# One two-block transformer kernel on one core: other load order, earlier scores, a split bias table, and a shorter last residual

## The chip, the core and the metric

The kernel runs on one core of a Trainium2 chip. The metric is device time in microseconds (us) of one execution. All data are float32, so every product on TensorE (PE) appears as two instructions in the profile. The other engines are VectorE (DVE), ScalarE (ACT), GpSimd (POOL) and SyncE (SP); SP, ACT and POOL issue DMAs. The memory the engines work in is SBUF; products arrive in PSUM.

## What is computed

256 tokens (2 tiles of 128), width 2048, go through two blocks.

```python
# first block, one layer
h = rms_norm(x, mix_norm_g);  proj = h @ w_in
y_a = causal attention of 16 heads from low-rank latents (rope on 64 of 192 dims)    # "mla"
y_b = causal attention of 16 heads with cumulative log forget gates                  # "fox"
x = x + (concat(y_a, y_b) * sigmoid(gates + b_gate)) @ w_out
h2 = rms_norm(x, ffn_norm_g)
# product keys: per token 8 heads x 16 experts out of 16384, found by two top-16 and a top-16 of sums
x = x + sum_k gate_k * gelu(h2 . peer_u[id_k]) * peer_v[id_k]
# second block, two layers
proj = x @ w_in
ya = difference of two softmaxes (4 heads), yb = dilated windows (8 heads), yc = conv of 31 taps
x = layer_norm(ALPHA * x + concat(ya, yb, yc) @ w_out, ln_g, ln_b)
```

Per tile 128 experts of each token are read twice (`peer_u`, `peer_v`): 256 gathers of 1 MB a tile, 512 in all.

## The kernel before

The order of passes on every engine is: `layer1(0)`, `experts(0)`, `layer1(1)`, `experts(1)`, then `layer2(l, t)` for (0,0), (1,0), (0,1), (1,1); `r = 2t + l + 1` numbers the last four as r = 1, 2, 3, 4. The argument of `layer1` and `experts` is the tile.

**Weights.** SP streams them in order (loop at L904) as units of 1 MB through a ring of four SBUF buffers. A unit is loaded as soon as PE has used the unit four before it. PE multiplies a unit in 4 products of 128x512 (8 instructions, L1242, L1276, L1284).

**Gathers.** POOL issues the 512 gathers in order (L866). Tile 0's need its expert numbers (`ids_ready`, from DVE at L695, in four rounds of 32). A gather goes into one of 6 or 7 row buffers and waits until DVE has used the buffer's last row (`row_used`). DVE uses a row in `slot()` (L356): a dot product with `hrow` (L362) for `peer_u`, a scaled addition to `x_sb` (L370) for `peer_v`. Slots are mixed into the other DVE work of the following passes: `stage(m)` fixes how many slots belong to a stage, `mix(f)` runs them up to the fraction f. DVE works in order, so a wait between two `mix` calls also holds back the slots, the freeing of rows, and POOL.

**experts(t)** (PE L1493, DVE L649, ACT L1100). PE transposes x to `hT`, multiplies it by the query weights in four chunks of four units, transposes each chunk (`keys_T`, L1501) and multiplies it by the sub keys (`scores`, L1510). Within chunk i it does units 0 and 1, `keys_T(i-1)`, units 2 and 3, `scores(i-1)`. DVE writes `hrow`, the normed row that the dot products use, from `x_sb`, the factor `rsh` and the row of gains `grow` (L665), runs the first stage of slots (`mix(1.0)`, none for tile 0, 10 for tile 1), and then takes the scores round by round (L674 to L695). `grow` is loaded once for each tile (`gain_row`, L1098), each time 1 MB, since one row of 8 KB goes to 128 partitions.

**Start.** SP loads tile 0 of x, waits for `k_in` (all constants and columns, L903), and streams the ring. ACT issues `konst`, `cols` and four small inputs (L964). PE's first transposes wait for x and `k_in`. ACT's first activation loads its function table when it comes.

**Second block.** DVE adds the masks `log_count` (`lnc`) to the whole bias table `bias2` at r = 1 (L769, L770). Both were loaded by ACT at the end of `layer1(1)` (L1094). For l = 1 the residual ALPHA * x enters the accumulation in PSUM by 16 products of `hT` with ALPHA times the identity (`residual()`, L1542). At a layer's end `add_out` (L519) takes each bank of 512 columns from PSUM, reduces it (L535) and sums the first three; ACT squares x minus a shift in two pieces (L1192, L1194); `layer_stats` (L541) makes mean and variance in five small operations, ACT takes the root (L1198), DVE the reciprocal (L554). At r = 3, ACT also loads the two rows of gains of the last norm (L1138, L1139, 1 MB each).

## Time and profile before

| | |
|---|---|
| median of 3 runs | 3245.87 us (3245.82 to 3246.41) |
| the profiled execution | 3247.37 us, its span 3245.6 us |
| PE busy | 2493.9 us (77%), 6764 instructions |
| DVE busy | 1670.2 us (51%) |
| ACT busy | 480.4 us (15%) |
| POOL busy | 938.7 us (29%) |
| bytes moved | 1192.41 MB, mean 367 GB/s |

The span begins with the first instruction and ends with the last; 1.77 us of the execution lie outside of it. A busy share is a mean over stages with different limits, so a change is weighed in the stage in which it lies: until about 580 us PE streams weights alone, to about 2642 us the gathers run beside it, and after that PE streams alone again. An instruction row of the trace gives start, duration, engine, line, what it writes and reads, and in brackets the idle time before it with what ended it.

### The profile page before, as it was taken

What the parts mean: (1) busy time and instruction counts of PE and PEld (TensorE: products, weight loads), DVE (VectorE), ACT (ScalarE), POOL (GpSimd) and SP (SyncE); (2) the same over time, 40 slices, a digit from 0 to 9 for tenths busy, and PEclk for the clock granted to TensorE, in tenths of its full rate; (3) what the DMA queues carried; (4) which work ended last, traced back from release to release, by engine and by line L of the source; (5) the groups of instructions that cost most, each with busy time, mean ns of one, the idle gap of its engine ahead of it and who ended that gap; (6) DMA issues with size and microseconds to landing.
All of it is one profiled execution on the core that took longest, in us unless ns stands there. A gap on an engine that the chain in (4) does not pass through costs nothing.

```text
span 3245.6 us, 19086 instructions
## 1 busy us (share of the span) xinstructions
PE 2493.9 (77%) x6764; PEld 1190.4 (37%) x6764; DVE 1670.2 (51%) x2188; ACT 480.4 (15%) x1159; POOL 938.7 (29%) x643
## 2 busy tenths in 40 slices
PE   8999999946847867576888267555745689999998
PEld 4444444413323333233433123222322234444553
DVE  1101112977576676676798956675985641011211
ACT  3222222111101111111101001010100011111211
POOL 0000000254354353343323334442342315300800
PEclk9999999977968878787999698778978899999999
DMA  8788787999999999999999999999999998887776
GB/s 319 268 294 279 271 285 273 394 421 421 421 416 420 422 419 422 422 417 422 410 421 421 405 422 422 421 415 422 421 402 422 421 392 284 280 287 268 269 265 220
DMA packets 166174, 1192.41 MB, mean 367 GB/s; under 512 B 18488, under 2 KB 18744, under 8 KB 21952
## 3 DMA queue, kind: packets, MB, share of 16 engines
q1 hardware_dynamic: 90320, 644.13, 52.6%
q0 software_dynamic: 73872, 537.95, 40.0%
q10 hardware_dynamic: 1888, 9.11, 0.7%
q8 instruction: 54, 0.88, 0.1%
q14 instruction: 40, 0.33, 0.0%
HBM read 1189.02 MB, written 2.10 MB: 367 GB/s over the span
## 4 chain that ended last, share of the span: by engine, by line
PE 40%; DMA 37%; DVE 14%; POOL 5%; issue 4%; ACT 1%; DVEq 0%; ACTq 0%
PE psP L1242 27%; DMA rows<-in_peer_v,tk 19%; DMA rows<-in_peer_u,tk 15%; PE psO L1276 6%; POOL rows L866 4%; DVE x_sb L370 4%; DVE rows L362 3%; DMA ring<-in_w 2%; PE psO L1284 2%; DVE work L386 1%; PE psX L1335 1%; PE psX L1332 1%; PE psX L1331 1%; POOL hrow L866 1%; DMA hrow<-in_peer_u,tk 1%
## 5 line engine op out<-in xcount | busy, mean ns | idle before, releaser
L1242 PE MATMUL psP<-ring,hT 128*128 128x512 f32 x3584 | 1633.0, 609 | 113.2 <-DMA ring<-in_w 106.1
L1242 PEld LDWEIGHTS psP<-ring,hT 128*128 128x128 f32 x3584 | 682.3, 195 | 978.8 <-issue 799.5
L866 POOL DMA_INDIRECT rows<-in_peer_u,tk x222 | 351.8, 1585 | 1091.8 <-DVEq L695 580.2
L370 DVE SCALAR_TENSOR_TENSOR x_sb<-rows,tk,x_sb 128x2048 f32<-128x2048 f32 x223 | 524.3, 2351 | 240.5 <-DMA rows<-in_peer_v,tk 220.4
L362 DVE CUSTOM_DVE_ANT_0 rows<-rows,hrow 128x2048 f32<-128x2048 f32 x222 | 503.9, 2290 | 193.7 <-DMA rows<-in_peer_u,tk 189.1
L866 POOL DMA_INDIRECT rows<-in_peer_v,tk x223 | 337.6, 1514 | 554.6 <-DVE x_sb L370 496.6
L1276 PE MATMUL psO<-ring,work 128*128 128x512 f32 x832 | 388.2, 620 | 0.5 <-DMA ring<-in_w 0.5
L1276 PEld LDWEIGHTS psO<-ring,work 128*128 128x128 f32 x832 | 162.3, 201 | 186.8 <-issue 186.0
L1368 PE MATMUL psX<-kst,work 128*128 128x128 f32 x128 | 26.9, 348 | 251.7 <-DVEq L517 194.9
L981 ACT ACTIVATE work<-work,small 128x256 f32<-128x256 f32 (+1 forms) x128 | 56.6, 443 | 482.9 <-DVEq L496 482.9
L514 DVE SCALAR_TENSOR_TENSOR work<-psX,small,work 128x128 f32<-128x128 f32 x96 | 27.0, 344 | 191.7 <-PE psX L1358 191.3
L1242 PE MATMUL psP<-ring,work 128*128 128x512 f32 (+1 forms) x288 | 114.8, 547 | 7.3 <-DMA ring<-in_w 7.3
L1368 PEld LDWEIGHTS psX<-kst,work 128*128 128x128 f32 x128 | 19.2, 176 | 273.1 <-DVEq L517 204.0
L370 DVE SCALAR_TENSOR_TENSOR x_sb<-hrow,tk,x_sb 128x2048 f32<-128x2048 f32 x33 | 77.6, 2351 | 36.5 <-DMA hrow<-in_peer_v,tk 33.1
L362 DVE CUSTOM_DVE_ANT_0 hrow<-hrow 128x2048 f32<-128x2048 f32 x34 | 77.8, 2290 | 28.1 <-DMA hrow<-in_peer_u,tk 27.4
L1335 PE MATMUL psX<-kv,work 128*128 128x128 f32 x128 | 28.0, 341 | 81.2 <-DVE kv L503 81.2
L1284 PE MATMUL psO<-ring,work 128*128 128x512 f32 x192 | 87.1, 611 | 1.7 <-ACT work L994 1.4
L866 POOL DMA_INDIRECT hrow<-in_peer_u,tk x34 | 54.5, 1604 | 89.1 <-DVE tk L362 67.9
L885 POOL TENSOR_TENSOR work<-work 128x512 f32<-128x512 f32 x60 | 76.2, 1271 | 4.7
L1242 PEld LDWEIGHTS psP<-ring,work 128*128 128x128 f32 x288 | 53.5, 190 | 64.7 <-issue 61.3
L866 POOL DMA_INDIRECT hrow<-in_peer_v,tk x33 | 50.0, 1517 | 85.6 <-DVE x_sb L370 73.4
L386 DVE SCALAR_TENSOR_TENSOR work<-work,cols 128x128 f32<-128x128 f32 x240 | 68.0, 346 | 0.0
(334 smaller groups left out, 1606.6 us busy)
## 6 DMA issues: line engine op xcount, KB each, us to landing
ring<-in_w SPq DMA_DIRECT2D x572, 1024.0 KB
ring<-in_wq SPq DMA_DIRECT2D x32, 1024.0 KB
ring<-in_w SPq DMA_DIRECT2D x8, 512.0 KB
rows<-in_peer_v,tk POOLq DMA_INDIRECT x223
rows<-in_peer_u,tk POOLq DMA_INDIRECT x222
x_sb<-in_x SPq DMA_DIRECT2D x2, 1024.0 KB, 6.4
rows<-in_gate_bias SPq DMA_DIRECT2D x1, 2048.0 KB, 12.7
work<-in_sub_keys ACTq DMA_DIRECT2D x2, 1024.0 KB, 9.2
```

The costliest lines, as they stand in the source:

```text
L362: V.tensor_tensor_reduce(out=row_buf(n), in0=row_buf(n), in1=hrow[:, t, :], scale=1.0, scalar=0.0, op0=ALU.mult, op1=ALU.add, accum_out=do ...
L370: V.scalar_tensor_tensor(out=x_sb[:, t, :], in0=row_buf(n), scalar=dots[t][:, k:k + 1], in1=x_sb[:, t, :], op0=ALU.mult, op1=ALU.add).then ...
L386: own.add(V.scalar_tensor_tensor(out=cacc[:, c, :], in0=convh[:, c, k:k + P], scalar=w, in1=cacc[:, c, :], op0=ALU.mult, op1=ALU.add))
L866: pool.indirect_dma_start(out=row_buf(n), out_offset=None, in_=a["peer_u" if s < SLOTS else "peer_v"], in_offset=bass.IndirectOffsetOnAxis ...
L885: own.link(T(cacc, cacc, csq, ALU.add))
L981: ins = A(W4[:, j, :], W4[:, j, :], ACT.Exp, bias=negm[:, 4 * u + j:4 * u + j + 1], accum_out=lsum[:, 4 * u + j:4 * u + j + 1])
L1242: last = MM(psP[:, c % 2, 0:wide], src[:, kk, :], w[:, k, :], start=(kk == 0 and not begun), stop=(kk == 4 * nu - 1))
L1276: last = MM(psO[:, d, :], src[:, k, :], w[:, d, :], start=(bool(first) and k == 0), stop=False)
L1284: last = MM(psO[:, d, :], src[:, k, :], w[:, k, :], start=False, stop=(k == 3))
L1331: MM(o, qT[:, j, :], kT[:, j, :], start=True, stop=False)
L1335: last = MM(o, qT[:, j, :], kT[:, j, :], start=(kind != "fox"), stop=(kind != "fox" or bank_ends))
L1368: last = TR(psX[:, 0, P * j:P * (j + 1)], mN[:, P * j:P * (j + 1)], ident)
```

## The change

1. Start: ACT loads only the identity and 16 columns first (`first_in`) and makes one activation of a constant that DVE has set (`booted`). The rest of `konst` and `cols` and the four small inputs are issued by POOL after x is there. SP no longer waits before the ring.
2. `experts`: `keys_T(i-1)` comes after one unit of chunk i and `scores(i-1)` after two. For tile 1, PE transposes `hT` back to rows in chunk 1 (`rows_back`), and DVE writes `hrow` from PSUM, before the first `mix`; the second load of `grow` is gone.
3. Bias table: columns 128 to 255 are loaded and masked where all were; columns 0 to 127 are loaded by ACT at r = 3 and masked by DVE there. ACT loads two more rows (gain and offset of layer 0's norm) behind them.
4. Tile 1's residual: at r = 3 DVE multiplies x by ALPHA, at r = 4 by ALPHA and the gains, and adds the offset; `residual()` is for tile 0 alone.
5. Statistics: for tile 1 addition and sum are one instruction; the second piece of the squares enters in ACT's root.

```diff
@@ vector
+                    sum_ = msum[:, d:d + 1]
+                    if t == 1:
+                        link(V.tensor_tensor_reduce(out=xv, in0=xv, in1=psO[:, d, :], scale=1.0, scalar=0.0, op0=ALU.add, op1=ALU.add,
+                                                    accum_out=sum_))
+                        dve.sem_inc(x_added, 1)
                     else:
...
-                link(V.tensor_scalar(vart[:, 1:2], nm, sh, None, ALU.subtract))
...
-                link(V.tensor_scalar(var, ssl[:, 0:1], ssl[:, 1:2], 1.0 / D, ALU.add, ALU.mult))
-                link(V.tensor_scalar(var, var, vart[:, 1:2], 1e-5, ALU.add, ALU.add))
+                link(V.scalar_tensor_tensor(out=bias, in0=ssl[:, 0:1], scalar=1.0 / D, in1=dev, op0=ALU.mult, op1=ALU.add))
...
                 take_xT(split, "ffn_g", (2, 3))
-                dve.wait_ge(grow_in, 16 * (t + 1))
                 dve.wait_ge(rsx_ready, t + 1)
+                if t == 0:
+                    dve.wait_ge(grow_in, 16)
                 for d in range(4):
                     w = slice(512 * d, 512 * (d + 1))
+                    if t == 1:
+                        dve.wait_ge(h2T_done, d + 1)
+                        V.tensor_scalar(hrow[:, 1, w], psX[:, d % 2, :], rsh[:, 1:2], None, ALU.mult).then_inc(h2T_taken, 1)
+                        continue
...
                 own.own()
+                if t == 1:
+                    dve.wait_ge(h2T_taken, 4)
                 mix(1.0)
...
                     layer_end(1, 0, 2)
+                    link(V.tensor_scalar(x_sb[:, 1, :], x_sb[:, 1, :], ALPHA, None, ALU.mult))
+                    dve.wait_ge(bias_in, 64)
+                    add_mask(slice(0, P), lnc_far)
+                if r == 4:
+                    link(V.scalar_tensor_tensor(out=x_sb[:, 1, :], in0=x_sb[:, 1, :], scalar=ALPHA, in1=ln_g0, op0=ALU.mult, op1=ALU.mult))
+                    link(V.scalar_tensor_tensor(out=x_sb[:, 1, :], in0=ln_b0, scalar=ALPHA, in1=x_sb[:, 1, :], op0=ALU.mult, op1=ALU.add))
@@ gpsimd
+            pool.wait_ge(x_in, 16)
+            pool.dma_start(kst[:, P:NKONST], a["konst"][:, P:NKONST]).then_inc(k_in, 16)
+            pool.dma_start(cols[:, DC:NCOLS], a["cols"][:, DC:NCOLS]).then_inc(k_in, 16)
+            for dst, name in ((rowc[:, :], "rowc"), (posi, "positions"), (dlam, "diff_lambda"), (work[32:40, 8448:9984], "gate_bias")):
+                pool.dma_start(dst, a[name]).then_inc(in_in, 16)
@@ sync
             sp.dma_start(x_sb[:, 0, :], a["x"][:, 0, :]).then_inc(x_in, 16)
-            sp.wait_ge(k_in, 32)
@@ scalar
+                act.dma_start(kst[:, 0:P], a["konst"][:, 0:P]).then_inc(first_in, 16)
+                act.dma_start(cols[:, 0:DC], a["cols"][:, 0:DC]).then_inc(first_in, 16)
+                act.wait_ge(booted, 1)
+                own.link(A(vart[:, 5:6], vart[:, 4:5], ACT.Copy))
...
-                    gain_row(1)
-                    act.dma_start(bias2, a["bias_t"]).then_inc(bias_in, 16)
-                    act.dma_start(lnc, a["log_count"]).then_inc(bias_in, 16)
+                    act.dma_start(bias2[:, :, P:S], a["bias_t"][:, :, P:S]).then_inc(bias_in, 16)
+                    act.dma_start(lnc, a["log_count"][:, :, P:S]).then_inc(bias_in, 16)
...
+                    act.dma_start(bias2[:, :, 0:P], a["bias_t"][:, :, 0:P]).then_inc(bias_in, 16)
+                    act.dma_start(lnc_far, a["log_count"][:, :, 0:P]).then_inc(bias_in, 16)
+                    for dst, name, at_ in ((ln_g, "ln_g", D), (ln_b, "ln_b", D), (ln_g0, "ln_g", 0), (ln_b0, "ln_b", 0)):
+                        act.dma_start(dst, bass.AP(tensor=a[name].tensor, offset=at_, ap=[[0, P], [1, D]])).then_inc(lnrow_in, 16)
...
-                A(vart[:, 2:3], vart[:, 0:1], ACT.Sqrt).then_inc(sd_ready, 1)
+                A(vart[:, 2:3], ssl[:, 1:2], ACT.Sqrt, scale=1.0 / D, bias=vart[:, 0:1]).then_inc(sd_ready, 1)
@@ tensor
-                    units(c, 0, 2, 4, hT)
-                    keys_T(i - 1)
-                    units(c, 2, 4, 4, hT)
-                    scores(i - 1)
+                    units(c, 0, 1, 4, hT)
+                    if t == 1 and i == 1:
+                        rows_back(0, 2)
+                        units(c, 1, 2, 4, hT)
+                        rows_back(2, 4)
+                        pe.wait_ge(h2T_taken, 4)
+                        keys_T(0)
+                        units(c, 2, 3, 4, hT)
+                        scores(0)
+                        units(c, 3, 4, 4, hT)
+                    else:
+                        keys_T(i - 1)
+                        units(c, 1, 2, 4, hT)
+                        scores(i - 1)
+                        units(c, 2, 4, 4, hT)
...
+                    for j in range(4):
+                        last = TR(psX[:, r % 2, P * j:P * (j + 1)], hT[:, 4 * r + j, :], ident)
+                    last.then_inc(h2T_done, 1)
...
-                        if l and g == 1:
+                        if l and t == 0 and g == 1:
                             residual()
```

## Rows read from the trace of the kernel before

**Rows 1.** The page's second part: GB/s moved in 40 equal slices.

```profile
GB/s 319 268 294 279 271 285 273 394 421 421 421 416 420 422 419 422 422 417 422 410 421 421 405 422 422 421 415 422 421 402 422 421 392 284 280 287 268 269 265 220
```

**Rows 2.** Stretches: us, busy of PE, PEld, DVE, ACT, POOL; clock, DMA share, GB/s.

```profile
560.00:580.00 20.00, 20.00 (x63) 10.13 (x62) 15.84 (x62) 1.97 (x3) 0.00 (x0) 1.00 0.82 280
1600.00:1700.00 100.00, 79.03 (x197) 34.95 (x196) 94.63 (x233) 9.53 (x14) 37.38 (x19) 0.95 1.01 422
580.00:2640.00 2060.00, 1338.59 (x3468) 629.51 (x3466) 1477.92 (x1748) 233.82 (x581) 793.95 (x512) 0.84 1.01 418
```

**Rows 3.** Waits over the span: who waited for what, us in total, times, longest.

```profile
DVE x_sb L370 <- DMA rows<-in_peer_v,tk: 220.4, 101, 2.7
```

**Rows 4.** Timeline of the start: start us, us, engine, line, operation, count, idle before.

```profile
7.42 25.29 SPq L909 DMA_DIRECT2D ring<-in_w  x9
7.51 1.57 PEld L1254 LDWEIGHTS psX<-kst,x_sb 128*128 128x128 f32 x8 [7.51 <-DMA x_sb<-in_x]
8.72 1.28 ACT L959 ACT_TABLE_LOAD   x1 [8.72 <-PE psX L1254]
12.31 0.50 PEld L1242 LDWEIGHTS psP<-ring,hT 128*128 128x128 f32 x2 [0.39 <-DMA ring<-in_w]
28.96 0.69 ACT L1013 ACTIVATE work<-psP,small 128x512 f32<-128x512 f32 x1 [4.76 <-PE psP L1242]
```

**Rows 5.** Timeline of `experts(0)`: first scores, DVE's copy of them, first gather.

```profile
562.12 1.05 PE L1510 MATMUL psO<-work 128*128 128x128 f32 x8
563.29 0.69 DVE L674 COPY rows<-psO 128x512 f32<-128x512 f32 x1 [21.67 <-PE psO L1510]
580.61 1.16 POOL L866 DMA_INDIRECT rows<-in_peer_u,tk  x1 [580.16 <-DVEq L695]
```

**Rows 6.** Timeline of `experts(1)`: PE, DVE and POOL up to the first scores.

```profile
1549.51 17.43 PE L1242 MATMUL psP<-ring,hT 128*128 128x512 f32 x40
1553.82 2.74 DVE L665 SCALAR_TENSOR_TENSOR hrow<-x_sb,small,kv 128x512 f32<-128x512 f32 x4 [8.21 <-ACTq L1117]
1556.59 17.09 DVE L370 SCALAR_TENSOR_TENSOR x_sb<-rows,tk,x_sb 128x2048 f32<-128x2048 f32 x7
1559.21 3.00 POOL L866 DMA_INDIRECT rows<-in_peer_v,tk  x1 [34.19 <-DVE x_sb L370]
```

**Rows 7.** Stretches around POOL's stop in `experts(1)`, columns as in rows 2.

```profile
1550.00:1555.00 5.00, 5.00 (x13) 2.28 (x12) 1.19 (x2) 3.60 (x7) 0.00 (x0) 1.00 1.01 422
1560.00:1565.00 5.00, 5.00 (x13) 2.19 (x12) 4.79 (x3) 0.69 (x1) 4.39 (x3) 1.00 1.01 324
```

**Rows 8.** DVE's waits from 1756 to 1800 us: us in total, times, longest.

```profile
DVE rows L362 <- DMA rows<-in_peer_u,tk: 10.5, 7, 1.6
DVE hrow L362 <- DMA hrow<-in_peer_u,tk: 2.3, 2, 1.5
```

**Rows 9.** Timeline: starved ring, then r = 3; last a load's KB and us to landing.

```profile
1583.58 3.70 PE L1242 MATMUL psP<-ring,hT 128*128 128x512 f32 x8 [0.84 <-DMA ring<-in_wq]
1588.57 3.70 PE L1242 MATMUL psP<-ring,hT 128*128 128x512 f32 x8 [1.29 <-DMA ring<-in_wq]
...
2650.09 58.76 PE L1242 MATMUL psP<-ring,hT 128*128 128x512 f32 x136
2675.61 0.69 DVE L741 TENSOR_TENSOR work<-work 128x512 f32<-128x512 f32 x1 [16.06 <-ACT work L1141]
...
rows<-in_ln_b ACTq DMA_DIRECT2D x1, 1024.0 KB, 11.1
```

**Rows 10.** Timeline of the boundary from r = 3 to r = 4, and `residual()`.

```profile
2934.81 0.69 DVE L535 TENSOR_REDUCE small<-x_sb 128x1 f32<-128x512 f32 x1
2937.81 1.38 PE L1254 MATMUL psX<-kst,x_sb 128*128 128x128 f32 x8 [3.87 <-DVE x_sb L819]
2940.99 5.76 PE L1242 MATMUL psP<-ring,hT 128*128 128x512 f32 x8
3082.06 3.74 PE L1545 MATMUL psO<-kst,hT 128*128 128x128 f32 x32
```

More of the change, by code:

```diff
@@ L264, in build @@
         bias2 = v3(kv[:, 6144:9216], S)
-        lnc = v3(kv[:, 2048:2560], S)
+        lnc = v3(kv[:, 2048:2304], P)
+        lnc_far = v3(rows[:, 4, 0:256], P)
         eid = [tk[:, 384 * t:384 * t + P].bitcast(U32) for t in range(TT)]
@@ L272, in build @@
         topk_home = [rows[:, NB - 1, :], kv[:, 0:2048]]
-        grow = [rows[:, NB - 1, :], kv[:, 4096:6144]]
+        grow = rows[:, NB - 1, :]
         skT = v3(wk(3840, 5888), NK)
-        ln_g, ln_b = rows[:, 0, :], rows[:, 1, :]
+        ln_g, ln_b, ln_g0, ln_b0 = (rows[:, m, :] for m in range(4))
         def row_buf(n):
@@ L544, in layer_stats @@
-                link(V.tensor_scalar(nm, msum[:, 3:4], part3[:, t:t + 1], 1.0 / D, ALU.add, ALU.mult))
-                link(V.tensor_scalar(vart[:, 1:2], nm, sh, None, ALU.subtract))
-                link(V.scalar_tensor_tensor(out=vart[:, 1:2], in0=vart[:, 1:2], scalar=-1.0, in1=vart[:, 1:2], op0=ALU.mult, op1=ALU.mult))
+                nm, sh, dev, bias = nmean[:, t:t + 1], shift[:, t:t + 1], vart[:, 1:2], vart[:, 0:1]
+                link(V.tensor_scalar(nm, msum[:, 3:4], part3[:, t:t + 1], -1.0 / D, ALU.add, ALU.mult))
@@ L557, in layer1 @@
                 stage(MIX1[0] if t else 0)
+                if t == 0:
+                    V.memset(vart[:, 4:5], 1.0).then_inc(booted, 1)
+                    dve.wait_ge(first_in, 32)
                 take_xT(split, "mix_g")
@@ L712, in finish_rows, with add_mask @@
                 dve.sem_inc(x_final, 1)
+            def add_mask(w, count):
+                own.add(V.tensor_tensor(bias2[:, 0:4, w], bias2[:, 0:4, w], over(count[:, 0, :], 4), ALU.add))
+                link(V.tensor_tensor(bias2[:, 4:12, w], bias2[:, 4:12, w], over(count[:, 1, :], 8), ALU.add))
             def apply_ln(t):
                 if t == 0:
-                    dve.wait_ge(lnrow_in, 32)
+                    dve.wait_ge(lnrow_in, 64)
                 for d in range(4):
@@ L768, in layer2 @@
                         dve.wait_ge(bias_in, 32)
-                        own.add(V.tensor_tensor(bias2[:, 0:4, :], bias2[:, 0:4, :], over(lnc[:, 0, :], 4), ALU.add))
-                        link(V.tensor_tensor(bias2[:, 4:12, :], bias2[:, 4:12, :], over(lnc[:, 1, :], 8), ALU.add))
+                        add_mask(slice(P, S), lnc)
                     mix(at_kT)
@@ L1192, in layer_squares @@
                 own.add(A(junk[:, 0:1536], x_sb[:, t, 0:1536], ACT.Square, bias=shift[:, t:t + 1], accum_out=ssl[:, 0:1]))
-                act.wait_ge(x_added, 8 + 4 * r)
-                own.add(A(junk[:, 1536:2048], x_sb[:, t, 1536:2048], ACT.Square, bias=shift[:, t:t + 1], accum_out=ssl[:, 1:2]))
                 own.own()
                 act.sem_inc(sq_done, 1)
+                act.wait_ge(x_added, 8 + 4 * r)
+                own.link(A(junk[:, 1536:2048], x_sb[:, t, 1536:2048], ACT.Square, bias=shift[:, t:t + 1], accum_out=ssl[:, 1:2]))
                 act.wait_ge(var_ready, r)
-                A(vart[:, 2:3], vart[:, 0:1], ACT.Sqrt).then_inc(sd_ready, 1)
+                A(vart[:, 2:3], ssl[:, 1:2], ACT.Sqrt, scale=1.0 / D, bias=vart[:, 0:1]).then_inc(sd_ready, 1)
             def y_count(l, t):
```

48 lines of the change are left out of this document (27 added, 21 removed).

## The prediction

> **What bounds the kernel now.** I read the page's slices first, then the stretches, then the waits, then the timeline at each place that the change touches. The slices show three stages [rows 1]. Up to slice 7 the DMAs move 268 to 319 GB/s and in the last seven slices 220 to 287; there PE streams weights and the transfers keep up. Between them, from 580 to 2640 us, they move 418 GB/s on average, in the busy stretches 421 to 422 [rows 2]; 422 is the most this kernel gets. DVE waits 220 us for rows of peer_v alone, 101 times [rows 3]. So the middle is a matter of bytes: 512 gathers and the ring share one pipe, and the stage ends when all of it is moved. There time is lost only where the pipe isn't full, and gained only where bytes go or where the pipe had room. DVE is a close second in places, 94.6% busy from 1600 to 1700 us [rows 2]. In the first and third stage a microsecond on PE's path is a microsecond of the total; a shift at the start moves everything behind it.
>
> **1, the start.** Now SP's ring, PE and DVE begin at 7.4 to 7.5 us, when x and all constants are there: 2.0 MB have come together [rows 4]. PE's first product of weights starts at 12.31, 4.8 us later; 1.28 us of that is ACT's table load, which sits between PE's first transposes and the first copy of them. After the change x is first in SP's queue with the ring behind it, and only 72 KB come beside it on ACT's. The nearest row for "first of several 1 MB loads on an idle queue" is the ring's first unit: issued at 7.42, landed by 12.31, 4.89 us [rows 4]. x, issued at 0.75, is then there at 5.6. Add 4.8 - 1.28 = 3.5 us: first product at 9.2, with unit 0 landed about 2.5 us behind x (1.05 MB at 422 GB/s), at 8.2. Gain 3.1 us. Bounds: 1.3 us if x lands no earlier than now and only the table load goes; 3.6 as the best. The Trainium skill, page "DMA: Bandwidth & Descriptors", section "Anatomy of one DMA", gives a fixed 2.0 us plus bytes over 436 GB/s for a load issued by GpSimd; as an estimate that is 4.4 us for x and would make the gain 3.6, while the row has 4.9, which I take. POOL's six loads (0.9 MB) start behind x. Who waits for them: DVE's rope work and ACT's Ln, behind which ACT's copies of PE's chunks are queued. The loads should land by 13 to 14 us (0.9 MB at half the pipe behind x), and ACT has 4.76 us of idle time before the first copy, at 28.96 [rows 4]; beyond that each microsecond is one of PE's. POOL has nothing else to do until 580. SP's later loads (x of tile 1, gate bias) keep their place.
>
> **2a, scores earlier in experts(0).** The first scores start at 562.12 [rows 5] and move two units up. A unit is 8 of the 136 instructions that take 58.76 us [rows 9], 3.46 us, so they move by 6.9, less the small waits of the transposes: 6.7. DVE idles 21.67 us for them and POOL waits for DVE's first round, so the first gather goes from 580.6 to 573.9. But from 560 to 580 us the pipe carries 280 GB/s [rows 2], so starting early uses (422 - 280) x 6.7 = 0.95 MB of room, 2.2 us. The other 4.5 us of lead only let the gathers take from the ring what they give back later. Bounds 0 and 6.7; I take 2.2. In experts(1) the earlier scores bring nothing: DVE takes them behind its ten slots.
>
> **2b, hrow of tile 1 from PSUM.** This is the part that costs. Now DVE waits for the factor until 1553.8, writes hrow in 2.74 us, and starts the slots at 1556.6; POOL, stopped for 34.2 us, resumes at 1559.2 [rows 6]. After the change the last two pieces come from rows_back(2, 4), behind two units of chunk 1. PE's 40 instructions from 1549.5 are the last three units of chunk 0 and two of chunk 1 [rows 6]; the first of chunk 1 ends at 1563.4. Add eight transposes (1.1 us, as the eight instructions of the scores in rows 5), a unit (3.4), four transposes (0.5), two copies from PSUM (1.4, as DVE's in rows 5): the slots begin at 1570. All behind it on DVE, and POOL behind DVE, is 13.4 us late. With gathers stopped the pipe falls from 422 to 324 GB/s [rows 7], or 280 with the ring alone [rows 2]; 13.4 us at 98 to 142 GB/s less is 1.3 to 1.9 MB, 3.1 to 4.5 us; I take 4.0. DVE's own lag of 13.4 us is not the price as long as DVE gets it back: from 1600 to 1700 it has little room, but from 1756 to 1800 it waits 12.8 us for rows [rows 8]. Bounds: 0, if later stretches with room in the pipe take it up (418 against 422 over 2060 us is 20 us of room [rows 2]), and 13.4. PE's 16 added transposes (2 us) lie where PE is starved.
>
> **3, bytes moved out.** grow's 1 MB and half of bias and mask (0.9 MB), together 2.0 MB or 4.7 us of pipe, leave the middle stage. They were moved while the gathers stood: the pipe is full to 1555 with them [rows 7], and PE ran without waiting for the ring. Take them away and it runs dry sooner; nothing else is ready to be moved. I count 0; bounds 0 and -4.7. DVE's two mask operations halve (1.8 us less at 1708), within a stretch whose time goes to row waits later: 0.
> At r = 3 ACT now issues 5.1 MB at once instead of 2.1. Two queues share evenly: with gathers beside it PE gets a unit every 5.0 us (3.70 busy, 1.29 waiting), against 3.4 used, and this starvation first shows about 23 us after the gathers resume [rows 6, 9]. The 2.1 MB of before landed within 11.1 us and PE's 136 instructions ran through [rows 9]. 5.1 MB at 210 GB/s take 24 us, 1.5 more than the ring holds out, at (5 - 3.4)/5 lost: 0.5 us. The half tables come in pieces of 512 bytes, which no row shows. If they cost double it is 28.5 us and 1.8 us lost. I take 0.9, bounds 0 and 4. The Trainium skill, "DMA: Bandwidth & Descriptors", section "Specifications", has 512 B as the least size at line rate; by it the term would be 0.5. DVE's new wait for the table has the gate of the convolution behind it, which now comes at 2675.61 after 16 us of idle time; PE asks for it behind the 136 instructions, at 2708.8: 33 us of cover [rows 9].
>
> **4, the residual.** 32 instructions, 3.74 us [rows 10], a little overlapped with their neighbours, on PE's path with nothing beside it: -3.6. DVE's added multiplications (2.4 us each, as one of the seven in rows 6) lie ahead of the same gate as above, under the same cover.
>
> **5, statistics.** At the end of r = 3 and r = 4 the reduction (0.69 us and its gap, L535) leaves the chain from the last bank to PE's restart at 2937.81 [rows 10]; five small operations stay five. 0.7 us each, -1.4. PE then idles 3.2 instead of 3.87 us; its clock fell to 1.2 GHz behind that gap and the first unit took 5.76 instead of 3.43 [rows 10]. If the shorter gap spares that, 2.3 more; I don't count it.
>
> **Sum.** -3.1 - 2.2 + 4.0 + 0 + 0.9 - 3.6 - 1.4 = -5.4 us. The terms are from the profiled execution of 3247.37 us, 1.5 above the median; from the median, 3245.87 - 5.4 = **3240.5 us**.
>
> **Rivals.** (a) DVE, not the pipe, carries the middle: the 13.4 us of 2b arrive whole. It decides if DVE isn't rid of its lag by 1800, when its row waits end. For it: DVE busy 94.6% in the stretch behind [rows 2]. Against: the 12.8 us [rows 8]. 3240.5 + 9.4 = 3249.9, slower than before; with the long burst of part 3, 3253. (b) The same for 2a: the 6.7 us arrive whole, 3236.0. Against: the row waits [rows 3], which a full pipe makes. (c) The 2.0 MB do count, since the rows that are under way at the stop land sooner and later dips take the rest: 3235.8. (d) x lands no earlier because the ring behind it crowds it, so the start does not do what it says: only the table load is gained, 3242.3.
>
> **Chances.** Forecast 0.45, (a) 0.20, (b) 0.12, (c) 0.13, (d) 0.10. 0.2% (6.5 us) is about what a measurement of this kernel tells from no change. Faster than 3239.4: (b), (c) and two fifths of the forecast's case, 0.42; slower than 3252.4: half of (a) and a little for what I don't see, 0.13; between them 0.45. Range 3232 (b or c together with a little more) to 3251 (a).
>
> **What the profile after would show.** PE's first L1242 at about 9.2 us. POOL's first gather some 10 us earlier than 580.6. In experts(1) POOL idle some 13 us longer than 34, and a stretch near 280 to 320 GB/s for 25 us around it; then DVE without row waits until it has caught up, or, by (a), x_final and everything behind it 13 us late relative to the start of the pass. No wait for the ring around 2680, or a few of 1.3 us. L1545 only for tile 0. The gap of PE between r = 3 and r = 4 down to 3.2 us. I am wrong if the whole stretch of the gathers, now some 2060 us [rows 2], differs by more than 5 us from the +8.5 that the terms give (first gather earlier by 6.7, less 2.2, plus 4.0).

## The result, and the profile after

The changed kernel takes 3252.06 us (median of 22 runs, 3246.89 to 3259.22) where the kernel before takes 3246.28 us in the same session (22 runs, 3243.59 to 3251.68). The ratio is 1.0018, with a 95 % interval of 1.0011 to 1.0024: 5.8 us slower. I had said 3240.5, range 3232 to 3251. The profiled execution took 3250.77 us, its span 3248.9 us, against 3247.37 and 3245.6 us for before. These two lie 3.4 us apart and the medians 5.8 (after's execution is 1.3 us below its median, before's 1.1 above), so the rows below account for 3.4 us; the other 2.4 us have no rows.

| Where | before, us | after, us | loss (+) or gain (-) of the stage |
|---|---|---|---|
| first transposes of experts(0) | 531.4 | 528.4 | -3.0 |
| first gather | 580.6 | 570.7 | (9.9 earlier) |
| first transposes of experts(1) | 1543.0 | 1537.2 | -2.8 |
| x of tile 0 final, layer2(0,0) begins | 1620.1 | 1627.7 | +13.3 |
| r = 3 begins | 2644.4 | 2646.8 | -5.1 |
| r = 4 begins | 2937.8 | 2946.5 | +6.3 |
| end of the span | 3245.6 | 3248.9 | -5.4 |

Two places lose: experts(1), and r = 3. Each has its rows.

The start. Timeline after (start us, us, engine, line, operation, count, idle before), which answers to [rows 4]:

```profile
1.19 0.45 ACTq L1000 DMA_DIRECT2D cols<-in_cols  x1
1.67 1.28 ACT L1002 ACT_TABLE_LOAD   x1 [1.67 <-PEq L1812]
8.81 1.94 PE L1289 MATMUL psX<-kst,x_sb 128*128 128x128 f32 x8 [8.81 <-DMA cols<-in_cols]
12.12 4.18 PE L1277 MATMUL psP<-ring,hT 128*128 128x512 f32 x8
```

The loads of the first 30 us after (KB, us from issue to landing):

```profile
x_sb<-in_x SPq DMA_DIRECT2D x1, 1024.0 KB, 5.2
kst<-in_konst ACTq DMA_DIRECT2D x1, 64.0 KB, 5.4
cols<-in_cols ACTq DMA_DIRECT2D x1, 8.0 KB, 7.5
```

x, issued at 0.75, is there at 5.95, 0.35 us behind the forecast. But PE waits until 8.8 for 8 KB of `cols`. The first product starts at 12.12, not at 9.2; what is gained is that ACT's table load is out of the way and that the first unit takes 4.18 us instead of the 5.87 in the same view of before. That this is TensorE's clock is a guess from the durations: the profile's rows grant 1.00 in both kernels from 12 to 18 us, and over the kernels below the first unit took 3.9 to 5.6 us with part 1 and 4.7 to 6.3 without, so single values say little.

The middle. Timeline after, first gather and experts(1), which answers to [rows 5, 6]:

```profile
1521.73 16.12 ACTq L1128 DMA_DIRECT2D kv<-in_log_count  x1
1537.89 0.63 ACT L1138 ACTIVATE hrow<-x_sb 128x512 f32<-128x512 f32 x1 [16.61 <-issue]
1540.96 0.63 PE L1289 MATMUL psX<-kst,x_sb 128*128 128x128 f32 x4 [2.75 <-issue]
1559.03 1.04 PE L1576 MATMUL psX<-kst,hT 128*128 128x128 f32 x8
1563.98 1.41 DVE L679 TENSOR_SCALAR hrow<-psX,small 128x512 f32<-128x512 f32 x2 [2.82 <-PE psX L1576]
1568.10 3.00 POOL L894 DMA_INDIRECT rows<-in_peer_v,tk  x1 [47.87 <-DVE x_sb L371]
```

POOL stands for 47.9 us, 13.7 more than in [rows 6], about as forecast, though by luck in part, since it has a second cause. The first line was not forecast: ACT's instruction that issues the load of the counts takes 16.12 us. The same load took ACT 0.45 us in before. (16.61 us is ACT's idle time before its first square; `issue` means that the profile shows nothing it waited for.) All ACT work of experts(1) is behind it, and PE waits 2.75 us for ACT's copies between its x transposes (0.84 in before).

What that does to the pipe, in stretches of after (us, busy of the engines, clock, DMA share, GB/s):

```profile
1540.00:1590.00 50.00, 47.97 (x147) 23.86 (x148) 23.31 (x14) 11.11 (x27) 17.68 (x8) 1.00 0.85 313
1590.00:1700.00 110.00, 80.70 (x207) 36.39 (x206) 102.55 (x272) 9.23 (x13) 39.26 (x21) 0.92 1.01 414
1540.00:1700.00 160.00, 128.68 (x353) 60.26 (x354) 125.87 (x285) 20.34 (x40) 56.95 (x29) 0.95 0.96 382
```

and the same 160 us of before:

```profile
1540.00:1700.00 160.00, 134.22 (x351) 60.78 (x350) 133.30 (x303) 21.64 (x43) 54.86 (x29) 0.97 1.01 416
```

(416 - 382) GB/s x 160 us = 5.4 MB were not moved. 1.97 MB of them (gain row, half table, half counts) no longer had to be, so 3.5 MB are owed to the rest of the middle stage: at 422 GB/s 8.2 us. Measured from the first transposes of experts(1) to the start of r = 3, after takes 1109.6 us and before 1101.4: 8.2 us. From x_final (x of tile 0 complete) to r = 3 after is the quicker by 5.1 us; both kernels move 418 GB/s there, so after simply has fewer bytes left, having moved more of them in its longer experts(1).

Then r = 3. Timeline of PE after, which answers to the third line of [rows 9] (there 136 instructions without a wait):

```profile
2677.74 3.67 PE L1277 MATMUL psP<-ring,hT 128*128 128x512 f32 x8 [1.07 <-DMA ring<-in_w]
2682.63 3.70 PE L1277 MATMUL psP<-ring,hT 128*128 128x512 f32 x8 [1.22 <-DMA ring<-in_w]
2688.85 29.43 PE L1277 MATMUL psP<-ring,hT 128*128 128x512 f32 x64 [2.52 <-DMA ring<-in_w]
```

4.8 us in three waits; behind the last the granted clock, 1.00 from 2660 to 2685, is 0.86 over ten microseconds (2690 to 2700), and the 64 instructions take 29.43 us where 64 of the 136 in [rows 9] take 27.65: 1.8 us. The sum, 6.6 us, less the 0.7 of the shorter statistics, is the stage's loss but for 0.4 us. The loads that shared the pipe with the ring (r = 3 of after; KB, median us from issue to landing):

```profile
rows<-in_ln_g ACTq DMA_DIRECT2D x2, 1024.0 KB, 18.1
rows<-in_ln_b ACTq DMA_DIRECT2D x2, 1024.0 KB, 22.5
kv<-in_bias_t ACTq DMA_DIRECT2D x1, 768.0 KB, 5.7
```

The last boundary, which answers to [rows 10]:

```profile
2946.51 1.11 PE L1289 MATMUL psX<-kst,x_sb 128*128 128x128 f32 x8 [3.14 <-DVE x_sb L847]
2949.69 4.84 PE L1277 MATMUL psP<-ring,hT 128*128 128x512 f32 x8
```

The gap is 3.14 us instead of the 3.87 of before, as forecast. The unit behind it takes 4.84 us instead of 5.76: the 0.9 us of clock that the forecast named and didn't count. The granted clock in before is 0.50, the level of 1.2 GHz, from 2940 to 2944 us. Over the ten microseconds behind the gap (the third number from the end) it is, before and then after:

```profile
2938.00:2948.00 10.00, 9.09 (x27) 4.85 (x27) 3.26 (x10) 3.01 (x8) 0.00 (x0) 0.66 0.09 16
2947.00:2957.00 10.00, 8.81 (x28) 4.64 (x27) 4.10 (x11) 3.01 (x8) 0.00 (x0) 0.83 0.19 52
```

### The profile page after: what moved, and what is told of

Read it like the earlier page. It is cut to its first block, busy times and chain, and to the rows that moved or that the text cites. A ratio compares the mean times of both kernels' runs of the same rounds, so it can differ in the third digit from the quotient of the medians.

```text
span 3248.9 us, 19075 instructions
## 1 busy us (share of the span) xinstructions
PE 2484.9 (76%) x6748; PEld 1186.3 (37%) x6748; DVE 1668.8 (51%) x2194; ACT 481.0 (15%) x1160; POOL 933.4 (29%) x649
## 4 chain that ended last, share of the span: by engine, by line
DMA 18%; PE 18%; DVE 11%; issue 3%; POOL 2%; ACT 0%; DVEq 0%; ACTq 0%
PE psP L1277 13%; DMA rows<-in_peer_v,tk 10%; DMA rows<-in_peer_u,tk 7%; DVE x_sb L371 3%; PE psO L1311 3%; DVE rows L363 2%; POOL rows L894 2%; DVE work L387 1%; PE psO L1319 1%; DMA ring<-in_w 1%; DMA hrow<-in_peer_u,tk 1%; DVE hrow L363 1%; PE psX L1393 0%; POOL hrow L894 0%; DVE kv L651 0%
## 5 line engine op out<-in xcount | busy, mean ns | idle before, releaser
L894 POOL DMA_INDIRECT rows<-in_peer_u,tk x222 | 344.0, 1549 | 1085.6 <-DVEq L713 561.0
L1289 PE MATMUL psX<-kst,x_sb 128*128 128x128 f32 x112 | 20.4, 329 | 65.8 <-DVE x_sb L847 33.6
```

The source lines that it names most:

```text
L894: pool.indirect_dma_start(out=row_buf(n), out_offset=None, in_=a["peer_u" if s < SLOTS else "peer_v"], in_offset=bass.IndirectOffsetOnAxis ...
```

## The experiments

Each was timed in 11 runs (two of them in 8 and 10) against runs of the kernel before on the same chip; times are medians, ratios come with their 95 % intervals. An interval reaches about 3 us to either side, so a difference of medians under 3 us can't be told from nothing by the times alone. The last three columns are from one profiled execution of each kernel. A kernel named "only" is the kernel before with one part of the change; one named "no" is the changed kernel without that part. Two columns of the table that follows carry the argument: "slots", from experts(1)'s first transposes to DVE's first slot behind the stop, and "middle", from the same point to the start of r = 3. The two profiled kernels have 13.6 and 1101.4 (before), 28.3 and 1109.6 (after).

| Kernel | Parts | us (before beside it) | ratio | slots | middle | r = 3 |
|---|---|---|---|---|---|---|
| only_1 | 1 | 3246.1 (3247.4) | 0.9996 [0.9987, 1.0005] | 13.6 | 1103.2 | 293.4 |
| only_2a | 2a | 3245.3 (3247.1) | 0.9991 [0.9982, 1.0000] | 13.6 | 1102.8 | 293.2 |
| only_2b | 2b | 3253.2 (3247.0) | 1.0020 [1.0010, 1.0029] | 26.8 | 1107.7 | 293.7 |
| only_3 | 3 | 3255.6 (3247.4) | 1.0027 [1.0018, 1.0036] | 22.4 | 1110.7 | 294.3 |
| counts_first | 3, other order | 3247.3 (3246.7) | 0.9998 [0.9989, 1.0007] | 13.6 | 1102.5 | 294.3 |
| only_45_late | 4, 5 | 3240.5 (3247.1) | 0.9983 [0.9974, 0.9992] | 13.6 | 1100.6 | 292.4 |
| no_2b | 1, 2a, 3, 4, 5 | 3250.2 (3247.0) | 1.0008 [0.9999, 1.0017] | 24.0 | 1111.7 | 297.2 |
| no_3 | 1, 2, 4, 5 | 3247.9 (3247.0) | 1.0004 [0.9995, 1.0013] | 26.4 | 1109.7 | 295.8 |
| rows_late | all, loads spread | 3247.2 (3247.0) | 0.9996 [0.9987, 1.0005] | 30.9 | 1113.6 | 292.4 |
| early_whole | 1, 2, 4, 5, 2b earlier | 3240.5 (3247.1) | 0.9976 [0.9967, 0.9985] | 19.8 | 1107.2 | 293.7 |
| sum_1_2a_45 | 1, 2a, 4, 5 | 3238.2 (3247.1) | 0.9975 [0.9966, 0.9984] | 13.6 | 1102.1 | 292.5 |
| sum_swap | the same, start swapped | 3238.1 (3247.4) | 0.9971 [0.9962, 0.9980] | 13.6 | 1103.0 | 292.5 |
| sum_hold | the same, ring held | 3237.5 (3247.4) | 0.9971 [0.9962, 0.9981] | 13.6 | 1102.2 | 292.4 |
| all_mended | all, four mendings | 3238.8 (3246.7) | 0.9974 [0.9964, 0.9985] | 19.5 | 1103.1 | 292.4 |

The "middle" of one execution isn't sharp: the eight kernels with slots at 13.6, before among them, spread from 1100.6 to 1103.2, and a single number of that column means no more than that.

**Undoing 2b or 3.** no_2b loads the gain row again and writes hrow of tile 1 the old way; no_3 loads table and counts whole in layer1(1):

```
-                    if t == 1:
-                        dve.wait_ge(h2T_done, d + 1)
-                        V.tensor_scalar(hrow[:, 1, w], psX[:, d % 2, :], rsh[:, 1:2], None, ALU.mult).then_inc(h2T_taken, 1)
-                        continue
+                    gain_row(1)
```

> The changed kernel with 2b undone: hrow of tile 1 again from x, gain row and factor, the gain row loaded again (1 MB). Theory H (the longer stop of POOL empties the pipe): POOL's stop goes from 47.9 back to about 34 us, x_final comes 6 to 8 us earlier, of which some 2 are given back by 2640 us; the total falls by 5 us, to 3247. Rival P (the loads in pieces of 512 bytes hold ACT and the pipe, so the stop matters little): x_final moves by 2 us at most and the 1 MB costs 2.4 us, total 3251 to 3253.

```
-                    act.dma_start(bias2[:, :, P:S], a["bias_t"][:, :, P:S]).then_inc(bias_in, 16)
+                    act.dma_start(bias2, a["bias_t"]).then_inc(bias_in, 16)
```

> The changed kernel with part 3 undone: the whole bias table and counts are loaded in layer1(1) in rows of 1 KB and up, 4.2 MB in whole rows are left at the start of r = 3. Theory P (pieces of 512 bytes cost more than their bytes): ACT is no longer held for 16 us behind its issue at 1521, PE's x transposes in experts(1) wait 2 us less, and r = 3 loses nothing to the ring (4.2 MB at 210 GB/s take 20 us, less than the ring's 23 us of reserve): total down by 8, 3244. Rival B (the bytes of the burst count, not their pieces): r = 3 still waits for the ring about 3 us instead of 4.8 and the total falls by 2 to 3, to 3249.5; the 0.9 MB more in the middle could take 2 of that back.

Taken away singly, neither brings what theory H or P wanted. Against before they are 3.2 and 0.9 us slower where the changed kernel is 5.8, so 2.6 and 4.9 us are gained, each give or take 3 us. no_2b shows why. Its slots still come 10.4 us late, although rows_back is gone: with the gain row queued too, ACT is held for 20.95 us and PE waits 8.58 us between its x transposes. Theory H expected x_final 6 to 8 us earlier and POOL's stop at 34; they were 4.4 and 43.1. no_3 frees ACT (its three issues take 0.33 to 0.45 us again) and halves r = 3's waits, but 2b's own lag stays, slots at 26.4. Its ring waits, 2.6 us, are about what rival B said (3). The two faults delay the same slots, so taking one away leaves most of the lag that the other makes. The middle of no_3 is as long as after's (1109.7 and 1109.6 us): in the changed kernel, what the hold of ACT costs the middle is about what the 0.9 MB spared by part 3 give it. The waits of PE over r = 3 of no_3, with 4.2 MB of whole rows at its start:

```profile
PE psP L1272 <- DMA ring<-in_w: 2.6, 2, 1.4
```

**The burst of r = 3.** rows_late issues the four rows behind the gates of groups 0 and 1, so that only the half table and counts stand at the start:

```
+                    if r == 3 and g < 2:
+                        for dst, name, at_ in (((ln_g, "ln_g", D), (ln_b, "ln_b", D)), ((ln_g0, "ln_g", 0), (ln_b0, "ln_b", 0)))[g]:
+                            act.dma_start(dst, bass.AP(tensor=a[name].tensor, offset=at_, ap=[[0, P], [1, D]])).then_inc(lnrow_in, 16)
```

> The changed kernel with the four rows of gain and bias (4.2 MB) issued one and two groups later in r = 3, so that only the half table and counts (0.9 MB in pieces of 512 bytes) come at its start. Theory B (bytes): no wait for the ring and no fall of the clock at r = 3, 6.3 us less, 3246. Theory P (pieces): the half table alone still starves the ring, PE waits 1 to 3 us and the gain is about 3 to 4 us, 3248.5. In either case the time up to 2646 us is that of the changed kernel within 1 us.

Theory B: r = 3 takes 292.4 us instead of 299.7, without a wait for the ring. PE's 136 instructions run through, with 0.9 MB in pieces of 512 bytes in front of them:

```profile
2656.50 58.53 PE L1278 MATMUL psP<-ring,hT 128*128 128x512 f32 x136
```

So it is mostly the bytes, one kernel for each amount: 2.1 MB (before) no wait, 3.0 MB (only_3) 0.8 us, 4.2 MB (no_3) 2.6 us, 5.1 MB (after) 4.8 us. The total fell by 5.6 us against before's. The middle of the profiled execution was 4 us longer than after's, where I had expected 1 us: ACT was held for 16.93 us and the slots came at 30.9.

**Each part alone.**

> The kernel before with 2b alone: hrow of tile 1 from PSUM behind two units of chunk 1, the gain row of tile 1 not loaded. Theory H: POOL's stop grows by 9 to 14 us, x_final comes 7 us later and the total rises by 4 to 6 us, to 3251. By my blind sum (the pipe's loss alone) it rises by 4.0, to 3250. Rival P: the stop is harmless without the loads in pieces, total within 1.5 us of before.

2b alone costs 6.2 us, where theory H had 4 to 6. Its stretch and its restart:

```profile
1540.00:1700.00 160.00, 130.79 (x364) 61.59 (x362) 125.63 (x282) 20.60 (x40) 56.08 (x29) 0.95 0.97 394
1570.00:1575.00 5.00, 5.00 (x19) 2.79 (x18) 4.79 (x3) 0.00 (x0) 3.91 (x2) 1.00 0.45 133
```

22 GB/s less over 160 us is 3.5 MB, less 1.05 MB that needn't be moved: 2.5 MB or 5.9 us; the middle is 6.3 us longer. The slots come 13.1 us late, by the prediction 13.4. What I had wrong is the rate while the gathers stand: not 280 to 324 GB/s throughout, but, in steps of 5 us from 1550, 318, 282, 323 and then 267 and 133. The low steps are those in which PE does transposes and waits (3.94 us busy of 5 from 1565) and in which the first gather behind the stop has only just been issued (1570.8); that these are the reasons is argued, not tested.

> Part 3 alone on the kernel before: half of the bias table and counts at the start of r = 3, both halves in pieces of 512 bytes. Theory P: ACT is held 15 to 21 us by the issue of the counts at 1527 (0.45 in before), PE's second x transposes in experts(1) wait 3 to 9 us instead of 0.8, DVE's slots begin 4 to 8 us later than 1556.6 and x_final as much; at r = 3 3.0 MB (0.9 in pieces) cost nothing or one wait of 1.3 us; total 3249 to 3252. Rival: the 0.9 MB less in the middle pay for the hold (-2.2 us), total within 1.5 us of before.

Part 3 alone costs 8.2 us, the most of all. The prediction had 0.9, and the total is beyond the text above too (3249 to 3252; 3255.6). Timeline of ACT in only_3:

```profile
1525.27 0.63 ACTq L1101 DMA_DIRECT2D kv<-in_bias_t  x1
1525.93 21.05 ACTq L1102 DMA_DIRECT2D kv<-in_log_count  x1
1547.03 0.63 ACT L1112 ACTIVATE hrow<-x_sb 128x512 f32<-128x512 f32 x1 [22.02 <-issue]
```

> Part 1 alone on the kernel before. Blind sum: first product at 9.2 us and 3.1 us less, 3243.5. By the changed kernel's trace: first transposes at 8.8 to 9.2 us (the 8 KB of cols land 7.5 us after their issue), first product at 12.1 to 12.5 as before, but at a faster clock, experts(0) begins some 2 us earlier, and the total falls by 1 to 2 us, to 3245.5; rival: the pipe in the middle swallows this too, 0.

1.3 us, which can't be told from nothing. The eight kernels with part 1 and the ring not held begin experts(0) at 528.0 to 529.0 us, the six without it, before among them, at 529.1 to 532.6: 2.2 us between the means. The 3.1 of the prediction was too much.

> Part 2a alone on the kernel before: scores one unit behind the queries in both experts passes. The first gather comes 6.5 to 7 us earlier, at 574. Blind sum: only the pipe's room counts, -2.2, 3244. Rival: the 6.7 us arrive whole, 3239.5. Second rival: the ring waits it causes and the dips later take all of it, 0, 3246.5.

The first gather is at 574.89, 5.7 us ahead of [rows 5] although this execution began experts(0) 1.2 us later, so 6.9 earlier by itself. The median gains 1.8 us (forecast: 2.2); the interval reaches from 0 to 5.8 us, so it rules out the rival of 6.7 but not the one of 0. The rows do: from the first transposes of experts(0) to those of experts(1) the ten kernels with 2a take 1008.5 to 1010.7 us, the six without it 1011.1 to 1012.2, 2.7 us between the means.

> Parts 4 and 5 alone on the kernel before, the rows of gain and bias issued one and two groups later in r = 3 (the changed kernel needs two more of them). By the blind sum -3.6 for the residual and 0.7 for each of two boundaries, -5.0: 3241.5. With what the changed kernel's trace shows at the clock (first product behind the gap 4.8 us instead of 5.8) -6: 3240.5. Rival: the added multiplications on DVE or the rows' loads delay the gate of the convolution or take the pipe, and no more than 3 us are left: 3243.5.

6.6 us by the medians, 5.5 by the ratio, against 5.0 in the prediction. The r = 3 to r = 4 boundary of this kernel:

```profile
2934.21 1.11 PE L1269 MATMUL psX<-kst,x_sb 128*128 128x128 f32 x8 [3.14 <-DVE x_sb L833]
2937.39 4.85 PE L1257 MATMUL psP<-ring,hT 128*128 128x512 f32 x8
```

It is 3.14 and 4.85 us here too, where before has 3.87 and 5.76: the shorter gap is followed by a shorter stretch at 1.2 GHz, 0.9 us that I had left out of the sum.

**What holds ACT.** By then the open point was whether the pieces hold ACT or the order. counts_first is only_3 with the counts issued ahead of the other loads and the half table behind them all:

```
+                if t:
+                    act.dma_start(lnc, a["log_count"][:, :, P:S]).then_inc(bias_in, 16)
                 act.dma_start(skT, a["sub_keys"]).then_inc(sk_in, 16)
...
                     act.dma_start(bias2[:, :, P:S], a["bias_t"][:, :, P:S]).then_inc(bias_in, 16)
-                    act.dma_start(lnc, a["log_count"][:, :, P:S]).then_inc(bias_in, 16)
```

> Part 3 alone on the kernel before, as in only_3, but the 128 KB of counts are issued first of ACT's four loads at the end of layer1(1) and the half table in pieces of 512 bytes last, so that no load is issued behind it. Theory Q (an issue behind a load in many pieces holds ACT until that load is under way): no issue longer than 1 us, ACT's first square of experts(1) at the time of before, PE's second transposes wait 0.8 us again, slots by 1555, total 5 to 7 us below only_3, 3249.5 (0.8 and its clock left at r = 3). Rival R (the pieces themselves hold ACT, wherever they stand): the hold of 16 to 21 us moves to the issue of the table or of the gain row, total 3255 again.

```profile
1526.57 0.63 ACTq L1099 DMA_DIRECT2D kv<-in_log_count  x1
1527.24 0.61 ACTq L1100 DMA_DIRECT2D work<-in_sub_keys  x1
1527.88 0.45 ACTq L1106 DMA_DIRECT2D kv<-in_ffn_row  x1
1528.37 0.55 ACTq L1103 DMA_DIRECT2D kv<-in_bias_t  x1
```

Theory Q, and 2 us better than it had. The same four loads, the same pieces, and no issue over 0.63 us; the slots are back at 13.6, and 8.2 us have become 0.6. So one load issued behind the half table costs 8 us here, and the half table itself nothing that these runs can tell. The table lands 28.8 us after its issue, twice the bytes in whole rows took 22.3 in before; nobody waits for it.

The order alone isn't the condition, though. At r = 3 the other half of the table, again 768 KB in pieces of 512 bytes, has loads issued behind it in six kernels, and ACT is not held there. From after:

```profile
2661.42 0.56 ACTq L1171 DMA_DIRECT2D kv<-in_bias_t  x1
2662.00 0.73 ACTq L1172 DMA_DIRECT2D rows<-in_log_count  x1
2663.41 1.51 ACTq L1174 DMA_DIRECT2D rows<-in_ln_b  x1
```

1.51 us is the longest issue at r = 3 in any kernel. The table lands 5.7 to 5.9 us after its issue at r = 3, and 23.0 to 25.6 in the four kernels that hold ACT: there the sub keys, and in two of them the gain row, are ahead of it on ACT's queue and the pipe is full (422 GB/s from 1550 to 1555 in before [rows 7]), while at r = 3 nothing of ACT's is ahead of it and the pipe has room (294 GB/s from 2660 to 2665 in after). The hold is also longer where the gain row (1 MB) goes ahead of the table (20.95 and 21.05 us) than where it doesn't (16.12 and 16.93). So what the runs show is that the issue behind a load in many pieces waits where that load itself is slow to get moving. Which limit it waits at they don't show.

**Moving rows_back forward.** early_whole has part 3 undone, the rows spread, and the two halves of rows_back behind the third and the fourth unit of chunk 0:

```
                     units(c, q, q + 1, 4, hT)
+                    if back_to and q == 2:
+                        pe.wait_ge(*back[3])
+                        back_to(0, 2)
+                    if back_to and q == 3:
+                        back_to(2, 4)
```

> The changed kernel with the bias table loaded whole in layer1(1) (3 undone), the rows of gain and bias later in r = 3, and rows_back(0, 2) and rows_back(2, 4) put behind the third and the fourth unit of chunk 0, so that DVE's slots in experts(1) start about 7 us earlier (1556.5 instead of 1563.3 with 3 undone). Theory H: x_final 5 to 7 us earlier than 1627.3, r = 3 begins 2 to 4 us earlier than 2646.6, no ring wait: total 3239 to 3241. Rival: the stop of POOL is not what 2b costs (the 1 MB that is not moved and the dips behind it level it), r = 3 begins at 2646 again and only the ring wait is gained: 3244.

The slots came at 19.8 instead of no_3's 26.4, x_final 8.2 us sooner, the total at 3240.5. The profiled execution began r = 3 only 1.8 us sooner than no_3's, less than theory H asked; its stretch 1540 to 1700 moved 408 GB/s, by which the middle should be under 1 us longer than before's and not 5.8. Where those 5 us went I don't know.

**The start.** sum_1_2a_45 leaves out 2b and 3 and spreads the rows; the two others change its start alone.

> Parts 1, 2a, 4 and 5 alone on the kernel before: 2b and 3 undone, and the four rows of gain and bias issued one and two groups later in r = 3. If the loss of the changed kernel sits in 2b, in the pieces of 512 bytes and in the burst, and the rest adds up (start -3.0, tail -5.4 as read from the traces, 2a between 0 and -2.2), x_final comes by 1618 us, no ring wait at r = 3, and the median falls 8 to 10 us below before, to 3237.5. Rival: the middle gives back what the start and 2a bring, since its end is a matter of bytes that are moved at 418 GB/s in any case and the earlier gathers only take from the ring; then r = 3 starts at 2642 to 2644 and the total is 5 us below before, 3241.5.

9.0 us below before: the parts alone give 1.3 + 1.8 + 6.6 = 9.7. The rival, that the middle swallows the gains (5 us), lies just outside the interval of 5.2 to 11 us.

```
-                act.dma_start(kst[:, 0:P], a["konst"][:, 0:P]).then_inc(first_in, 16)
                 act.dma_start(cols[:, 0:DC], a["cols"][:, 0:DC]).then_inc(first_in, 16)
+                act.dma_start(kst[:, 0:P], a["konst"][:, 0:P]).then_inc(first_in, 16)
```

> Parts 1, 2a, 4 and 5 as in the sum kernel, with ACT's first two loads in the other order: the 8 KB of cols (pieces of 64 bytes) issued at 0.75, the 64 KB of konst at 1.2. Theory C (what is issued at 1.2 us lands behind the ring's first unit, whatever its size): konst lands at 8.7 and nothing is gained, first transposes at 8.8 to 9.1, total 3238. Theory D (the pieces of 64 bytes are slow by themselves, 7.5 us from issue): cols lands at 8.3, konst at 6.6, first transposes at 8.3 to 8.6, total 3237.5. If neither, both land with x at 6 to 6.5, first product at 9.7 and the total is 2 us lower, 3236.

```profile
kst<-in_konst ACTq DMA_DIRECT2D x1, 64.0 KB, 7.7
cols<-in_cols ACTq DMA_DIRECT2D x1, 8.0 KB, 5.5
```

```
             sp.dma_start(x_sb[:, 0, :], a["x"][:, 0, :]).then_inc(x_in, 16)
+            sp.wait_ge(first_in, 32)
```

> Parts 1, 2a, 4 and 5 as in the sum kernel, with SP's ring held until the two first loads have landed, so that only x is beside them. Theory C (crowded by the ring's first unit): cols lands at about 6.3 instead of 8.7, first transposes at 6.3, the ring's first unit is issued then and is there 4.9 us later, at 11.2, which is when the first product starts (12.4 in the sum kernel); total 1 us lower, 3237. Theory D (slow pieces): cols lands at 8.5 again, the ring's first unit at 13.5, and the total is 1 us higher, 3239.5.

```profile
6.89 1.94 PE L1280 MATMUL psX<-kst,x_sb 128*128 128x128 f32 x8 [6.89 <-DMA cols<-in_cols]
11.77 5.37 PE L1268 MATMUL psP<-ring,hT 128*128 128x512 f32 x8 [1.36 <-DMA ring<-in_w]
```

Theory C twice over. Swapped, the two loads swap their times: whatever is issued at 1.2 us, 8 KB or 64, lands 7.5 to 7.9 us later, behind the ring's first unit, which was issued at 1.19 too. With the ring held both need 5.6 us and the transposes start at 6.9. Then the ring's unit is the late one, and the first product comes 0.6 us sooner than in sum_1_2a_45. The median is 0.5 us below that of sum_swap on the same chip, which these runs can't tell from nothing. sum_hold is the fastest kernel of the study, 3237.5 us, 0.9971 of before.

**All parts, mended.** Ring held, counts first, rows_back forward, rows spread:

> All parts of the changed kernel with four things mended: SP's ring held until the two first loads are there, the counts issued ahead of the half table, rows_back behind the third and fourth unit of chunk 0, the four rows of gain and bias one and two groups later in r = 3. Theory Q: slots begin at about 1556, no ring wait at r = 3, total as that of early_whole with the start of sum_hold, 3239.5. If the 1 MB and 0.9 MB that it doesn't move in the middle count after all (4.7 us), 3236. Theory R: ACT is held again, slots at 1562 or later, total 3243.

3238.8 us, between the 3239.5 and the 3236 of theory Q; the four mendings were not tried one by one. Slots 5.9 us late, and yet the middle is only 1.7 us longer than before's: 12 GB/s less over 1540 to 1700 is 1.92 MB, and 1.97 MB needn't be moved. sum_hold, without 2b and 3, is at 3237.5 with an interval that overlaps: even mended, 2b and 3 bring nothing that can be told from nothing.

## Why the prediction was wrong

The steps that failed are the landing of `cols` at the start, the rate at which 2b loses bytes, the issue on ACT that part 3 makes slow, and the length and price of the burst at r = 3. In the order of the terms:

- **1, the start** (-3.1; measured -1.3 alone). x and the ring's first unit landed when they should (5.95 and 8.5 us for 5.6 and 8.2). The step that failed is "only 72 KB come beside it": I took them as there with x because they are small. They landed last, at 8.7 us, and the first product stayed at 12.1 instead of 9.2. (The prediction also has DVE begin at 7.4 to 7.5 us; in before it begins at 9.5, which no term uses.) Rival (d) had the ring crowd x; it crowded `cols`.
- **2a** (-2.2; measured -1.8 by the median, -2.7 by the rows). Right: most of the 6.7 us of lead doesn't arrive. That it is the pipe's room between 560 and 580 us that counts fits, and was not tested by itself.
- **2b** (+4.0; measured +6.2 alone). The delay was right (13.1 for 13.4 us), and so was pricing it by missing bytes; the rate at which bytes go missing was mis-sized. In the terms of the sum: 3.5 MB missing less 1.05 saved, where I had 1.3 to 1.9 MB.
- **3, bytes** (0, bounds 0 and -4.7). Where both parts are in and 1.97 MB are spared, the stretch gives the middle only if they are taken off: 8.2, 12.8 and -0.1 us for after, rows_late and all_mended, measured 8.2, 12.2 and 1.7; without taking them off it would be 4.7 us more each. For 0.9 or 1.05 MB alone it stays open: only_2b (5.9 with them taken off, 8.3 without, measured 6.3) and no_3 (7.7, 10.2 and 8.3) speak for it, only_3 (7.7, 9.9 and 9.3), no_2b (7.7, 9.9 and 10.3), counts_first (-1.0, 1.1 and 1.1) and early_whole (0.5, 3.0 and 5.8) against. And nothing was left of the saving, since the stops that came with it cost more. I had written that the ring "runs dry sooner; nothing else is ready to be moved", and that is the other side of the same account.
- **3, the issue on ACT** (not in the sum; alone worth the 8.2 us of only_3 less the 0.6 of counts_first). This wait the prediction had at nothing without a reason. It asked what a moved DMA does to the ring and never what its issue does to ACT's own queue. Each issue of before takes 0.33 to 0.45 us there, and the prediction gave the issue no price at all. In the changed kernel it overlaps with 2b: without it (no_3) the slots come 26.4 instead of 28.3 us behind the first transposes.
- **3, the burst at r = 3** (+0.9, bounds 0 and 4; measured about 6.6 with the clock). Three sizes failed. I let the ring hold out 23 us, as it did behind POOL's restart; it held out 15, from the issue at 2661.4 to the first wait at 2676.7. The 23 us were a poor measure: in the first 15 us behind POOL's restart the ring of before was given 3.40 MB, at r = 3 of after 3.03 MB, and until its first wait before's PE did 2.2 us of transposes and scores, which use no unit. (Nothing shows that after's ring was behind when the burst came: its units issued at 2656.1 and 2659.5 landed in 5.0 and 5.3 us.) The burst lasted 30.5 us, until the last row landed at 2691.9, and not 24. By the prediction's own rate, (5 - 3.4)/5 of the 15.3 us beyond the reserve, that is 4.9 us, and 4.8 were measured. And I left out the clock behind a wait, although [rows 10] shows it, worth 1.8 us here.
- **4 and 5** (-5.0; measured -6.6 alone, -6.3 by the rows of r = 3 and r = 4). Right, with 0.9 us of the clock that I didn't count.

What turned the sign is not one of these steps alone. In the two profiled executions the middle has +8.2 us for the +4.0 of the sum, and r = 3 has +6.3 for +0.2 (0.9 less 0.7); the start and the tail came about as forecast there (-3.0, and -5.4 for -4.3). And with 2b, part 3 or the burst of four rows taken out singly, the changed kernel is 3.2, 0.9 and 0.2 us slower than before, never faster.

The rival (a) gave 3249.9, "with the long burst 3253", and the time is 3252.1. The number is near; the mechanism isn't its. (a) was to decide by DVE still carrying its lag at 1800 us. After's DVE waits for rows 7.8 us between 1756 and 1800 ([rows 8]: 12.8), so it had begun to have slack again, and yet the time was gone: the pipe had stood partly empty, and that isn't given back. My test for being wrong, the stretch of the gathers more than 5 us off +8.5, gives 2076.1 less 2063.8 = +12.3 and doesn't trip. It was too coarse: at -2.2 + 4.0 it asked for 1.8 us of loss in the middle and let 5.6 pass.

The singles add to -1.3 - 1.8 + 6.2 + 8.2 - 6.6 = +4.7, to which the burst of four rows is still to be added, while 2b and the hold of ACT delay the same slots and overlap. The changed kernel has +5.8.

## What to carry to other kernels

Where a stage is bound by a pipe, price a stop in bytes: what isn't moved in the stretch around it, less what no longer has to be, over the pipe's rate; that account gave the length of the middle within some 2 us for thirteen of the fifteen other kernels here; it missed no_2b by 2.6 and early_whole by 5 us. When a load is split into short pieces or moved, read the issue of the load behind it on the same engine as closely as its landing; while the pipe is full, put the load in pieces last. A small load on the critical path has to be issued before the large ones or have them held back; here its size, 8 or 64 KB, didn't help it.
